# PEER decoder block on one core: gates of the dense tokens added by indirect DMAs into a zeroed DRAM matrix in place of one-hot matmuls, with the lo parts of the U pass on VectorE

## The reference, cut to what matters

```python
def peer_ffn(h, w_q, sk1, sk2, eu, ev):            # 8 heads, 128 keys a side, 16384 experts
    q = (h @ w_q).reshape(B_, S_, 8, 2, 128)
    s1 = einsum('bshd,nd->bshn', q[..., 0, :], sk1)
    s2 = einsum('bshd,nd->bshn', q[..., 1, :], sk2)
    v1, i1 = top_k(s1, 16); v2, i2 = top_k(s2, 16)
    cand_s = v1[..., :, None] + v2[..., None, :]   # 256 candidates a head
    cand_i = i1[..., :, None] * 128 + i2[..., None, :]
    top_s, pos = top_k(cand_s, 16)
    eidx = take_along_axis(cand_i, pos)            # 8 x 16 experts a token
    g = softmax(top_s)
    a = gelu(einsum('ckd,cd->ck', eu[eidx], h)) * g
    return einsum('ck,ckd->cd', a, ev[eidx])
```

## Time and profile before

| | |
|---|---|
| Median of 3 runs | 1699.33 us (1699.23, 1699.33, 1705.9) |
| Span of the profiled execution | 1570.0 us |
| What lies around the span, against that median | 129.3 us |
| TensorE busy | 1532.5 us (98%), mean granted clock 0.986 |
| VectorE busy | 1302.3 us (83%) |
| ScalarE busy | 725.6 us (46%) |
| GpSimd busy | 1031.4 us (66%) |
| DMA | 444.68 MB, mean 283 GB/s |
| U pass, slabs 0 to 127 | about 404 to 788 us |
| V pass | about 800 to 1554 us |

### The profile page before, as it was taken

One profiled execution on the slowest core, in us unless ns is written; L12 is line 12 of the kernel. 1 busy time (PEld: TensorE's weight loads), 2 busy tenths in 40 slices (PEclk: granted clock), 3 DMA queues, 4 the chain that ended last, 5 costly groups with the idle time before them and its releaser, 6 DMA issues.

```text
span 1570.0 us, 23281 instructions
## 1 busy us (share of the span) xinstructions
PE 1532.5 (98%) x7942; PEld 1233.9 (79%) x7942; DVE 1302.3 (83%) x2291; ACT 725.6 (46%) x1177; POOL 1031.4 (66%) x724
## 2 busy tenths in 40 slices
PE   6999999899999999999999999999999999999998
PEld 5886668788887888888877787878777787877776
DVE  6496565578999899998978898898898889988987
ACT  4544432333445555555454444444444444444442
POOL 3542213243698777778967777777777777777770
PEclk8999999799999999999999999999999999999999
DMA  8334545332476889898978999999999999999993
GB/s 322 124 108 139 171 122 187 121 107 82 151 244 216 272 267 304 271 297 272 327 277 323 379 364 398 376 372 380 380 361 396 360 388 405 369 406 371 370 396 157
DMA packets 219589, 444.68 MB, mean 283 GB/s; under 512 B 22360, under 2 KB 128984, under 8 KB 219232
## 3 DMA queue, kind: packets, MB, share of 16 engines
q1 hardware_dynamic: 174432, 309.04, 56.7%
q0 software_dynamic: 45056, 134.38, 22.3%
HBM read 407.68 MB, written 35.67 MB: 282 GB/s over the span
## 4 chain that ended last, share of the span: by engine, by line
POOL 52%; issue 35%; PE 10%; DMA 1%; DVE 1%; POOLq 0%; ACT 0%; DVEq 0%; SPq 0%
POOL wlo L618 19%; POOL coef L658 16%; POOL rows L652 16%; PE ps L1771 2%; PE ps L1559 2%; PE ps L1476 1%; PE ps L1477 1%; PE ps L1475 1%; PE ps L1779 1%; PE ps L1781 1%; PE ps L1780 1%; DMA rows<-w_stream,row_at 1%; DMA ada<-w_ada 1%; PE ps L1537 0%; PE ps L1541 0%
## 5 line engine op out<-in xcount | busy, mean ns | idle before, releaser
L618 POOL TENSOR_TENSOR wlo<-raw,whi 128x1024 fp32r<-128x1024 f32 x178 | 435.4, 2462 | 317.3 <-ACT whi L689 316.9
L1475 PE MATMUL ps<-ahi,whi 128*128 128x256 f32 (+1 forms) x1296 | 397.8, 307 | 5.6 <-ACT gout L920 2.3
L1476 PE MATMUL ps<-alo,whi 128*128 128x256 f32 (+1 forms) x1296 | 395.5, 305 | 0.0
L1477 PE MATMUL ps<-ahi,wlo 128*128 128x256 f32 (+1 forms) x1296 | 395.5, 305 | 0.0
L652 POOL DMA_INDIRECT rows<-w_stream,row_at x256 | 288.9, 1128 | 87.5 <-issue 77.1
L658 POOL DMA_INDIRECT coef<-gelu_spill,coef_at x256 | 290.4, 1134 | 78.0 <-issue 78.0
L1409 DVE SCALAR_TENSOR_TENSOR ps<-rows,coef,ps 128x1024 f32<-128x1024 f32 x252 | 256.7, 1019 | 12.3 <-DMA rows<-w_stream,row_at 1.4
L1475 PEld LDWEIGHTS ps<-ahi,whi 128*128 128x128 f32 x1296 | 246.4, 190 | 22.3 <-ACT gout L920 2.5
L689 ACT ACTIVATE whi<-raw 128x1024 fp32r<-128x1024 f32 x176 | 186.2, 1060 | 160.6 <-PE ps L1725 93.1
L1476 PEld LDWEIGHTS ps<-alo,whi 128*128 128x128 f32 x1296 | 246.9, 190 | 15.4
L1477 PEld LDWEIGHTS ps<-ahi,wlo 128*128 128x128 f32 x1296 | 246.7, 190 | 10.8
(11 more groups left out here) (244 smaller groups left out, 2359.1 us busy)
## 6 DMA issues: line engine op xcount, KB each, us to landing
raw<-w_stream SPq DMA_DIRECT2D x304, 512.0 KB, 5.3
values_in<-w_stream SPq DMA_DIRECT2D x128, 512.0 KB, 7.4
ada<-w_ada SPq DMA_DIRECT2D x32, 512.0 KB, 4.4
gelu_spill<-gout SPq DMA_DIRECT2D x64, 256.0 KB, 5.5
gate_spill<-gblock SPq DMA_DIRECT2D x8, 2048.0 KB, 10.6
gates<-gate_spill SPq DMA_DIRECT2D x32, 512.0 KB, 9.0
ada<-w_ada SPq DMA_DIRECT2D x32, 256.0 KB, 7.2
rows<-w_stream,row_at POOLq DMA_INDIRECT x256, 7.6
```

Source lines behind the costliest of these rows:

```text
L618: g.tensor_tensor(wlo[:, s, :], raw[:, s, :], whi[:, s, :].bitcast(F32), ALU.subtract)\
L1475: mm(out, shi, mhi, start=n == 0, stop=False)
L1476: mm(out, shi, mlo, start=False, stop=False)
L1477: last = mm(out, slo, mhi, start=False, stop=n == len(pairs) - 1)
```

## The change

The matrix of gates is now in DRAM as `gate_rows`, 128 experts by 128 chunks by 256 tokens. SyncE clears it with 16 stores of 1 MB from a zeroed tile, 12 of them behind the last loads of the query projection's chunks and 4 behind the first slab loads. VectorE then makes the picks in five parts (heads 0 to 3 of tile 0, heads 4 to 7 of tile 0, tiles 1, 2 and 3), normalises the gates of each part at once, and for tiles 0 and 1 works out the place of each gate in the matrix (`place_gates`). GpSimd adds the gates: for each of 128 picks of a tile one indirect DMA with 128 elements, one of each token (`add_gate`). Two heads can pick the same expert for a token, so the 16 DMAs of a head wait for those of the head before in the same tile; `GATE_ORDER` gives four heads of tile 0, then the other four in turn with four of tile 1, then the last four of tile 1. Only then come the row and coefficient fetches. SyncE loads the first gates when all adds of both tiles have landed.

The one-hot products, their adds, their transposes and the stores of `gblock` are gone. GpSimd makes lo parts only for slabs 0 to 7; VectorE makes those of slabs 8 to 127, between the steps of the picks (`between`) and after them, and also those of the first two chunks of the V pass.

```diff
+U_POOL = 8
+HALF_LO, PICK_LO = 12, 23
+ZERO_PIECES = 16
+PICKS = [(0, range(HALF_HEADS)), (0, range(HALF_HEADS, PH))] + [(t, range(PH)) for t in range(1, TT)]
+GATE_ORDER = [(0, h) for h in range(4)] + [(t, h + 4 * (1 - t)) for h in range(4) for t in range(2)] \
+    + [(1, h) for h in range(4, 8)]
...
-    gate_dram = nc.dram_tensor("gate_spill", (NK // GROUP, P, BLOCKS, GROUP * TOK_BLOCK), F32).ap()
+    gate_dram = nc.dram_tensor("gate_rows", (P, NK, HALF), F32).ap()
```

On SyncE:

```diff
+            def clear_gates(n):
+
+                width = NK // ZERO_PIECES
+                if n == 0:
+                    sp.wait_ge(zeros_made, 1)
+                some = gate_dram[:, n * width:(n + 1) * width, :].rearrange("p (a b) n -> p a (b n)", b=RING)
+                sp.dma_start(some, zeros[:, :].unsqueeze(1).to_broadcast([P, width // RING, D])).then_inc(gate_zeroed, 16)
+
+            for n, c in enumerate(range(C_OUT + RING + DK, C_U)):
                 load_front(c)
+                clear_gates(n)
             for e in range(7):
-                load_slab(e // RING, e % RING, e % RING, C_U + e - RING + 1)
+                load_slab(e)
+                if e < RING:
+                    clear_gates(ZERO_PIECES - RING + e)
...
-                if e == U_C + 10:
-                    for b in range(2):
-                        sp.wait_ge(gate_stored[b], 16 * (BLOCKS // 2 + 1))
-                    for b in range(2):
-                        gate_load(b, b)
...
+            for t in range(PAIR):
+                sp.wait_ge(gate_landed[t], 16 * P)
+            for b in range(2):
+                gate_load(b, b)
```

On GpSimd:

```diff
-            with pool.Fori(2, C_E // RING) as i:
+            with pool.Fori(2, (C_U + U_POOL) // RING) as i:
...
+            def add_gate(t, n):
+
+                g.indirect_dma_start(gate_dram.rearrange("p i (n o) -> (p i n) o", o=1),
+                                     bass.IndirectOffsetOnAxis(gate_at[:, t, n:n + 1], 0),
+                                     picked[:, 2, t * P + n:t * P + n + 1], None, compute_op=ALU.add)\
+                 .then_inc(gate_landed[t], 16)
+
+            def add_head(t, h):
+
+                if h > 0:
+                    pool.wait_ge(gate_landed[t], 16 * TOPK * h)
+                elif t == 0:
+                    pool.wait_ge(gate_places, 1)
+                if h == HALF_HEADS and t == 0:
+                    pool.wait_ge(gate_places, 2)
+                if h == 0 and t == 1:
+                    pool.wait_ge(gate_places, 3)
+                for n in range(h * TOPK, (h + 1) * TOPK):
+                    add_gate(t, n)
+
+            pool.wait_ge(gate_zeroed, 16 * ZERO_PIECES)
+            for t, h in GATE_ORDER:
+                add_head(t, h)
             pool.wait_ge(places_ready, 1)
             for m in range(ROWS):
                 fetch_row(m)
```

On ScalarE:

```diff
-            for e in range(U_A2 // RING * RING, U_B):
+            for e in range(NK - RING):
                 u_step(e, e // RING, e % RING)
...
+                if e in EXP_AFTER:
+                    weights_exp(EXP_AFTER.index(e))
```

On VectorE:

```diff
+            v.memset(zeros[:, :], 0.0).then_inc(zeros_made, 1)
...
+            def slab_lo_parts(n):
+
+                for e in itertools.islice(slabs, n):
+                    dve.wait_ge(hi_ready, C_U + e + 1)
+                    v.tensor_tensor(wlo[:, e % RING, :], raw[:, e % RING, :], whi[:, e % RING, :].bitcast(F32),
+                                    ALU.subtract).then_inc(slab_lo_ready, 1)
...
+            def place_gates(t, heads):
+
+                first, second = (picked[:, k, slots_of(t, heads)] for k in range(2))
+                some = slice(heads[0] * TOPK, (heads[-1] + 1) * TOPK)
+                v.scalar_tensor_tensor(gate_expert[:, some], second, float(NK), first, ALU.mult, ALU.add)
+                dve.drain()
+                v.tensor_scalar(gate_place[:, some], gate_expert[:, some], float(HALF), token[:, t:t + 1], ALU.mult, ALU.add)
+                dve.drain()
+                v.tensor_copy(gate_at[:, t, some], gate_place[:, some]).then_inc(gate_places, 1)
+
+            dve.wait_ge(token_ready, 1)
+            dve.wait_ge(gate_zeroed, 16 * ZERO_PIECES)
+            for n, (t, heads) in enumerate(PICKS):
+                pick_experts(t, heads, (lambda parts: None, lambda parts: slab_lo_parts(1), slab_lo_parts)[min(n, 2)])
+                weights_normed(n, t, heads)
+                if t < PAIR:
+                    place_gates(t, heads)
+                dve.drain()
...
+            slab_lo_parts(NK)
```

On TensorE:

```diff
-            with pe.Fori(0, (U_C - U_B) // BODY_CHUNKS) as i:
-                for m in range(BODY_CHUNKS):
-                    u_slab(i * BODY_CHUNKS + (U_B + m), m)
-                    for j in groups_after(m):
-                        scatter(i * BODY_GROUPS + j, j)
+            with pe.Fori(U_POOL // RING, NK // RING) as i:
+                for s in range(RING):
+                    u_slab(i * RING + s, s, slab_lo_ready, 1 - U_POOL)
```

More of the change, by code:

```diff
@@ L347, in build @@
         gate_exp = sem("gate_exp")
[L348 to L351, removed]
+        zeros_made = sem("zeros_made")
+        gate_zeroed = sem("gate_zeroed")
+        gate_places = sem("gate_places")
+        gate_landed = [sem(f"gate_landed{t}") for t in range(PAIR)]
         gelu_done = sem("gelu_done")
@@ L416, in conv_taken, with slab_lo @@
             return ((cgate_ready, z_ready, yconv_ready)[n % 3], n // 3 + 1)
[L419 to L428, removed]
-            return both[:, :, part * NK:(part + 1) * NK].rearrange("p t n -> p n t")
+        def slab_lo(e):
+            return (lo_ready, e + (C_U + 1)) if e < U_POOL else (slab_lo_ready, e - (U_POOL - 1))
         block = ctx.enter_context(nc.Block())
@@ new lines, in slab_lo_parts, with slots_of, pick_experts @@
+            def slab_lo_parts(n):
[3 more added lines that the diff above has]
+                                    ALU.subtract).then_inc(slab_lo_ready, 1)
+            def slots_of(t, heads):
+                return slice(t * P + heads[0] * TOPK, t * P + (heads[-1] + 1) * TOPK)
+            def pick_experts(t, heads, between):
+                n = len(heads)
+                some = slice(heads[0], heads[-1] + 1)
+                values = top_v[:, t, :, :].rearrange("p (h s) a -> p h s a", s=2)[:, some, :, :]
+                second = second_v[:, 0:n, :]
+                v.tensor_copy(second, values[:, :, 1, :])
@@ L1239, in pick_experts @@
                 for k in range(2):
-                    v.tensor_copy(index_of[:, k, :, :],
-                                  top_i[:, t, :, :].rearrange("p (h k) a -> p k a h", k=2)[:, k, :, :])
+                    v.tensor_copy(index_of[:, k, :, 0:n],
+                                  top_i[:, t, :, :].rearrange("p (h k) a -> p k a h", k=2)[:, k, :, some])
+                between(2)
                 dve.drain()
-                for h in range(PH):
+                for h in range(n):
                     v.max(best[:, h, 0:8], cand[:, h, :])
+                    if h % 4 == 3:
+                        between(1)
@@ L1424, in prod_lo @@
                                 ALU.subtract).then_inc(plo_ready, 1)
+            for e in range(PAIRED):
+                again_lo(e)
             make_value_lo(0)
```

288 lines of the change are left out of this document (83 added, 205 removed).

## The result

The changed kernel takes 1894.11 us (median of 5 runs, 1889.77 to 1905.97); the kernel before, 1704.74 us beside it (5 runs, 1699.23 to 1721.01). Ratio 1.1146, 95% interval 1.1111 to 1.1182: **11% slower**. The forecast was slower, at 1750, with a range of 1683 to 1850; the result lies outside it.

The account below looks back on a forecast made before the run. TensorE was taken to pace both passes; late adds would move the first product of gates and gelus from 798.9 to 847, 48 us, plus 2 for the clock: 1699.3 + 50 = 1749, given as 1750, range 1683 to 1850.

Parts of the forecast that it names:

- the price of one add: GpSimd in the U pass: each indirect add costs 1.44 us like a coefficient fetch, 256 of them 368 us.
- Waits for landings: GpSimd between heads of adds: eight uncovered waits for the head before, 3.8 us each, 30 us in all.
- P0: First product of gates and gelus, forecast at 847 against 798.9; the new span is this plus 771.1 us.
- VectorE's delay: GpSimd's issue: a transfer starting just after VectorE's lo part lasts until that ends plus 0.8 us; mean 1.44 against 1.24.
- upper bound: All adds on GpSimd: 1.24 us each plus a delay of 1.0 for each of about 124 lo parts, 443 us.
- The place: SyncE's wait for all 256 landings before loading the first gates; TensorE idle from about 787, some 50 us.
- The hole at slab 8: TensorE early in the U pass: idle some 14 us, 426 to about 440, until VectorE makes the ninth lo part.
- 129.3 us outside the span; I take this as fixed: Whole kernel: median 1699.33 us against a profiled span of 1570.0; the difference stays, every term changes only the span.
- An add is dearer than a fetch: Rival, GpSimd's issue: grows by half, 0.94 to 1.41 us, 120 us in all, P0 967, 1869 us; chance 0.21.
- The adds end under the U pass: Rival, SyncE's wait: last landing by about 781, U pass bounds, P0 787, 1687 us, faster; chance 0.14.
- It cancels: Rival: adds at 1.24 to 1.3 us, P0 between 790 and 807, 1691 to 1708 us, no change; chance 0.10.
- The V pass slows: Rival, V pass gates loads: 128 KB pitch halves their rate, about 22 us on top, 1771; no separate chance.

Follow-up runs that it names:

- experiment 3: Changed kernel with the 256 indirect DMAs writing their gates instead of adding: 1614.7 us, ratio 1.0235 to the kernel before on the same chip.
- the other pitch: Changed kernel with the rows of an expert in the gate matrix 132 KB apart instead of 128: 1771.22 us, ratio 1.1245 to the kernel before.
- experiment 1: The kernel before, run again unchanged with its own profile: 1576.04 us on one chip (ratio 0.9996), 1693.51 us on another (ratio 1.0023).
- experiment 2: Changed kernel with expert rows 132 KB apart instead of 128, 1771.22 us (ratio 1.1245); changed kernel unchanged on another chip, 1889.04 us (1.1103).

## Why the prediction was wrong

**The step that failed is the price of one add.** "No such add is in the trace. The nearest rows are the fetches of single coefficients ... I take the mean of the rows, 1.44: 256 x 1.44 = 368 us." Measured: 2.10 each, 538.7 us, 170.7 more. Other terms gave a little back (all in us):

| Term | Forecast | Measured |
|---|---|---|
| First places | 436 | 438.25 |
| Adds with gaps | 368 | 538.7 |
| Waits for landings | 30 | 18.5 |
| Last add issued, landed, gates loaded, to P0 | 4 + 9 | 6 |
| P0 | 847 | 1001.56 |

170.7 + 2.2 - 11.5 - 7 = 154 us, and P0 is 154.6 late. Of the 0.67 us that each add was short, 0.60 are the accumulation (1.547 against 0.946 undisturbed), which the prediction put at nothing (experiment 3 removes it); 0.04 are VectorE's delay and 0.02 the gap. The "upper bound" of 443 us was none: it bounded fetches. It had counted the delay by VectorE in full and the new operation at nothing.

That the delay came out close is in part luck. The forecast took the V pass's 0.19 us a transfer (1134 against 946 ns), although it said itself that the U pass has twice as much of the cause. Under the U pass it measured 0.41 (1.96 against 1.55). The mean over all 256 adds is only 58.6 / 256 = 0.23, because 110 of them came so late that VectorE stood idle beside them.

**What held, point by point.** The place: SyncE's wait for the landings, with TensorE idle behind it. The hole at slab 8: forecast from 426 to 440, measured TensorE waiting 10.86 us up to 440.58. The U pass: forecast to end at 780, with TensorE idle from about 787; measured, its last matmul starts at 773.1 and TensorE stands before the V pass from 781. The places of the fetched rows: forecast 672, measured 662, not on the path. Eight waits for landings: forecast 3.8 us each, measured 2.3 on average. The V step: forecast 5.95 us, measured 5.96 on average with the other pitch on chip A. In the changed kernel's own profile the mean is 6.98, which the prediction had named as a sign of being wrong; half of its steps still take 5.97 or less, and 27 are over 8 us, as 33 are in the kernel before on chip C. Zeros: the last of their stores is issued at 385.1, VectorE waits for none of them, and the first add starts 2 us after the forecast.

**"129.3 us outside the span; I take this as fixed"** was wrong in what it is (experiment 1), and did no harm, since the same amount stood in the timed runs of both kernels: the change costs about as much wherever it ran, 194 us with the other pitch on chip A, 188 as it is on chip B and 189 in the first result.

**The rivals.** "An add is dearer than a fetch" was the right one, at a chance of 0.21: forecast 0.47 us more, P0 967; measured 0.6 more. It should have been the likeliest: the prediction itself says that the operation reads, adds and writes, and nothing in the trace spoke for the price of a plain fetch. Its 1869 us were still 25 short, and the measured time is 4 us above the 1800 to 1890 that went with it: it had taken half of 0.94 for the growth, where the accumulation adds 0.60. "The adds end under the U pass" has its point: half the adds do, 1.3% faster. "It cancels" needed 1.24 to 1.3 us an add. "The V pass slows" by the pitch: refuted by the V passes of experiment 2.

## What to carry to other kernels

An operation that the trace does not show has no bound from one that looks like it: an indirect DMA that adds cost GpSimd 1.55 us for 128 elements, one that writes 0.96 and one that fetches 0.94. Count the new instructions of a serial engine against the window that hides them, here some 140 of 256, before counting what the others save, and take their price in that window, not the mean over the whole run. And where the span of a profile is 8% below the timed runs, suspect that the profiled execution was a faster one, on another chip perhaps, before explaining the difference by work outside of it.

## What the runs showed of the hardware that was not expected

- The same kernel took 1577 us on one chip and 1694 to 1701 on two others, 8% apart, nearly all of it in the V pass (773 against 898 us), with a granted clock of 1.00 against 0.94 there. Each chip was used once, so that it is the chip and not the hour is not shown.
- A large VectorE operation on two SBUF tensors beside it lengthens GpSimd's issue of an indirect DMA: 2.22 us against 1.55 beside a lo part, up to 3.85, whichever of two operations makes it, and 2.47 beside a bf16 comparison. A product with one operand in PSUM and a reduction do not: 1.55.
- An indirect DMA of 128 elements makes 144 packets when it adds and 32 when it writes.
- Adds whose 128 elements are neighbours slow the other transfers: 150 GB/s against 237 in the same stretch of the U pass, and 96.6 us of waits for landings against 19.7. Scattered places, as the kernel has them, are the better case. Why was not tried.
